# Decay-gate products stacked over 96 rows, and first q and k projections started on three of six token tiles

## The reference, cut to what matters

```python
h = rmsnorm(x, norm_mix)
proj = h @ w_in                      # qa, ka, va, qb, kb, vb, og, gf, gb, ma, mb
logg_f = jax.nn.log_sigmoid(gf @ w_gate_f + b_gate_f) / GATE_TAU   # gf: [T, 16], w_gate_f: [16, 4 heads x 128]
logg_b = jax.nn.log_sigmoid(gb @ w_gate_b + b_gate_b) / GATE_TAU
o_f = gla_chunked(qb, kb, vb, logg_f, False)                      # per head, chunks of 64 tokens
o_b = flip(gla_chunked(flip(qb), flip(kb), flip(vb), flip(logg_b), True))
...
x = x + mix @ w_out
x = x + hier_moe(rmsnorm(x, norm_moe), ...)                       # 32 experts, two of them per token
return rmsnorm(x, norm_final)
```

## Time and profile before

| | us |
|---|---|
| median of 3 runs | 1326.04 |
| lowest, highest run | 1317.42, 1728.16 |
| the profiled execution | 1316.45 |
| its span, first to last instruction | 1314.3 |
| TensorE busy in the span | 1190.0 |
| VectorE, ScalarE, GpSimd busy | 645.2, 599.3, 338.8 |

### The profile page before, as it was taken

The page is one execution under the profiler, slowest core; times in us unless marked ns, Lnnn a source line. Parts: engine busy times, 40 slices in busy tenths (PEclk is TensorE's granted clock), DMA queues, the critical chain, the costliest instruction groups (busy, mean ns, idle before and its releaser), DMA issues.

```text
span 1314.3 us, 18331 instructions
## 1 busy us (share of the span) xinstructions
PE 1190.0 (91%) x7184; PEld 1059.7 (81%) x7184; DVE 645.2 (49%) x1056; ACT 599.3 (46%) x994; POOL 338.8 (26%) x214
## 2 busy tenths in 40 slices
PE   5999999998999999999999999889399999999960
PEld 3998898797877878899999999889377887777750
DVE  5001512327554444355302112325498998888857
ACT  6133645534534344133212213122467888877843
POOL 1221120121111112021112024230134554444510
PEclk8999999997899999999999999899689999999995
DMA  7621101322111111111121211501679999999917
GB/s 253 196 65 32 33 5 48 107 79 61 33 33 34 32 33 32 33 45 54 53 64 42 77 60 64 182 16 65 251 289 373 366 369 367 343 366 350 349 62 288
DMA packets 89941, 184.11 MB, mean 140 GB/s; under 512 B 14009, under 2 KB 65357, under 8 KB 81678
## 3 DMA queue, kind: packets, MB, share of 16 engines
q1 hardware_dynamic: 79486, 167.16, 35.7%
q0 software_dynamic: 10384, 15.95, 3.4%
HBM read 179.32 MB, written 28.65 MB: 158 GB/s over the span
## 4 chain that ended last, share of the span: by engine, by line
PE 69%; DVE 10%; DMA 7%; ACT 7%; issue 5%; POOL 1%; SPq 0%; POOLq 0%; ACTq 0%; DVEq 0%
PE bank L1256 16%; PE bank L1258 15%; PE bank L1257 15%; DMA raw_gu<-in_w_exp_up 5%; PE bank L1443 2%; PE bank L1442 2%; PE bank L1441 2%; PE bank L1390 2%; PE bank L1321 2%; ACT w_hi L1006 2%; PE bank L1365 2%; PE bank L1343 1%; PE bank L1428 1%; PE bank L1387 1%; PE bank L1304 1%
## 5 line engine op out<-in xcount | busy, mean ns | idle before, releaser
L881 POOL TENSOR_TENSOR w_lo<-raw,w_hi 128x2048 fp32r<-128x2048 f32 (+2 forms) x37 | 152.9, 4133 | 673.4 <-ACT w_hi L1006 673.3
L1256 PE MATMUL bank<-hT_hi,w_hi 128*128 128x384 f32 (+1 forms) x592 | 202.9, 343 | 4.0 <-DVE hT_lo L1580 4.0
L1257 PE MATMUL bank<-hT_lo,w_hi 128*128 128x384 f32 (+1 forms) x592 | 199.7, 337 | 0.0
L1258 PE MATMUL bank<-hT_hi,w_lo 128*128 128x384 f32 (+1 forms) x592 | 199.6, 337 | 0.0
L995 ACT ACTIVATE hi_gu<-raw_gu 128x2048 fp32r<-128x2048 f32 x64 | 122.4, 1918 | 62.9 <-issue 51.5
L1844 DVE TENSOR_TENSOR lo_gu<-raw_gu,hi_gu 128x2048 fp32r<-128x2048 f32 x64 | 146.3, 2287 | 6.3 <-ACT hi_gu L995 6.1
L1256 PE MATMUL bank<-w_hi,hT_hi 128*128 128x256 f32 x432 | 126.3, 292 | 0.0
L1257 PE MATMUL bank<-w_lo,hT_hi 128*128 128x256 f32 x432 | 123.4, 286 | 0.0
L1258 PE MATMUL bank<-w_hi,hT_lo 128*128 128x256 f32 x432 | 123.4, 286 | 0.0
L1006 ACT ACTIVATE w_hi<-raw 128x2048 fp32r<-128x2048 f32 (+2 forms) x42 | 73.6, 1752 | 103.0 <-PE bank L1258 103.0
L1256 PEld LDWEIGHTS bank<-hT_hi,w_hi 128*128 128x128 f32 (+1 forms) x592 | 111.3, 188 | 9.1 <-DVE hT_lo L1580 4.4
(11 more groups left out here) (291 smaller groups left out, 2544.7 us busy)
## 6 DMA issues: line engine op xcount, KB each, us to landing
raw_gu<-in_w_exp_gate SPq DMA_DIRECT2D x32, 1024.0 KB, 10.9
raw_gu<-in_w_exp_up SPq DMA_DIRECT2D x32, 1024.0 KB, 13.7
raw_down<-in_w_exp_down SPq DMA_DIRECT2D x32, 1024.0 KB, 14.8
raw<-in_w_in SPq DMA_DIRECT2D x25, 1024.0 KB, 5.6
y_pair<-y_d SPq DMA_DIRECT2D x12, 512.0 KB, 9.0
raw<-in_w_in SPq DMA_DIRECT2D x8, 512.0 KB, 5.8
raw<-in_w_proj_b SPq DMA_DIRECT2D x4, 1024.0 KB, 5.0
raw<-in_w_out SPq DMA_DIRECT2D x4, 1024.0 KB, 5.2
```

The lines of the kernel that those rows point to most:

```text
L881: pool.tensor_tensor(w_lo[:, g % 2, 0:kb, 0:n], raw[:, g % 2, 0:kb, 0:n], w_hi[:, g % 2, 0:kb, 0:n].bitcast(F32), ALU.subtract).then_inc(w ...
L1256: pe.matmul(out, l_hi, r_hi, start=j == 0, stop=False)
L1257: pe.matmul(out, l_hi, r_lo, start=False, stop=False)
L1258: ins = pe.matmul(out, l_lo, r_hi, start=False, stop=j == n - 1)
```

## The change

The gate's weight columns are loaded three times, so that its product has 96 rows: three copies of the 32. Evacuated, the rows become hi, lo and hi (ScalarE copies all 96, VectorE subtracts on the middle 32). A new step `wgz` makes the matching operand from a 96-row `wgate`: ScalarE copies all of it to `wgz`, VectorE replaces the last 32 rows by the rest. Then z is one `fp32r` matmul over 96 rows instead of a float32 matmul over 32. In the step list `wgz` stands right in front of z, and so behind the `w` step that ends the projection before it.

At the start the list is written out by hand: the first four products (q and k, token half 0) need only tiles 0 to 2 and stand between the transposes of tiles 3 to 5; the `w` steps of groups 0 and 1 move forward; group 0 is loaded before tiles 3 to 5, the replication of the bias vectors behind group 2's load. TensorE gets filler transposes of the identity (14 ahead of each of the first three tiles' transposes, 28 ahead of the first product), whose results are overwritten. The root of the norm takes its scale and bias on ScalarE, without VectorE's step.

```diff
+WARM = 14
+G2, G3 = 2 * RANK, 6 * RANK
...
-    for i in range(NT + 2):
-        if i < NT:
-            if i < NV:
-                steps.append(S(kind="vec", a=i))
-            steps.append(S(kind="norm", i=i))
-        if i == NT:
-            steps.append(S(kind="w", g=0))
-        if i >= 2:
-            steps += [S(kind="hT", i=i - 2, half=h) for h in range(2)]
-    steps.append(S(kind="w", g=1))
-    steps += proj("q", 0) + proj("k", 0) + proj("v", 0)
+    hT = lambda i: [S(kind="hT", i=i, half=h) for h in range(2)]
+    norm = lambda i: [S(kind="norm", i=i)]
+    vec = lambda a: [S(kind="vec", a=a)]
+    q, k = proj("q", 0), proj("k", 0)
+    early, late = ([s for s in q + k if s.kind == "w" or s.s == half] for half in range(2))
+    early = [s for s in early if s.kind == "ws"]
+    steps += vec(0) + norm(0) + vec(1) + norm(1) + hT(0) + vec(2) + norm(2) + hT(1) + [S(kind="w", g=0)] + hT(2)
+    steps += norm(3) + early[0:1] + hT(3) + norm(4) + [S(kind="w", g=1)] + vec(3) + early[1:2] + norm(5) + vec(4)
+    steps += hT(4) + early[2:3] + hT(5) + early[3:4] + late + proj("v", 0)
...
-    other = v[3:] + z
+    other = v[3:] + [S(kind="wgz", h=0)] + z
...
-        steps += other[i:i + 1]
+        steps += other[0:2] if i == 3 else other[0:1]
+        del other[0:2 if i == 3 else 1]
...
-            steps += [S(kind="z", h=h + 1, d=d, s=s) for d in range(2) for s in range(2)]
+            steps += [S(kind="wgz", h=h + 1)] + [S(kind="z", h=h + 1, d=d, s=s) for d in range(2) for s in range(2)]
...
-                return [(w_in[:, C_GATE:C_GATE + 2 * RANK], KD, 0, 2 * RANK)]
+                return [(w_in[:, C_GATE:C_GATE + G2], KD, c0, G2) for c0 in range(0, G3, G2)]
...
-            for i in range(1, NT):
+            for i in range(1, NT // 2):
+                sp.dma_start(xin[:, i, :], x_rows(i)).then_inc(x_in[i], 16)
+            load_group(0)
+            for i in range(NT // 2, NT):
                 sp.dma_start(xin[:, i, :], x_rows(i)).then_inc(x_in[i], 16)
...
+                    if s.g + 1 < len(glist):
+                        if s.g:
+                            need(sp, E_, wlo_done, s.g)
+                        load_group(s.g + 1)
+                    if s.g == 1:
                         replicate_vectors()
...
-                        need(pool, E_, mm, find(kind="z", h=h - 1)[-1].job + 1)
-                    pool.dma_start(wgate[0:RANK, 0, :], ...
-                    pool.dma_start(wgate[RANK:2 * RANK, 1, :], ...
+                        need(pool, E_, wgz_done, h)
+                    for c0 in range(0, G3, G2):
+                        pool.dma_start(wgate[c0:c0 + RANK, 0, :], ...
+                        pool.dma_start(wgate[c0 + RANK:c0 + G2, 1, :], ...
...
-                    need(act, E_, var_done, i + 1)
-                    act.activation(std[:, i:i + 1], rstd[:, i:i + 1], ACT.Sqrt).then_inc(std_done, 1)
+                    need(act, E_, consts, 2)
+                    need(act, E_, sq_done, i + 1)
+                    act.activation(std[:, i:i + 1], ss[:, i:i + 1], ACT.Sqrt, scale=1.0 / D, bias=eps[:, 0:1])\
+                       .then_inc(std_done, 1)
...
+                elif k == "wgz":
+                    need(act, E_, wg_in, 96 * (s.h + 1))
+                    if s.h:
+                        need(act, E_, mm, find(kind="z", h=s.h - 1)[-1].job + 1)
+                    act.activation(wgz[:, :, :], wgate[:, :, :], ACT.Copy).then_inc(wgz_hi, 1)
+                elif k == "ws" and s.dest[0] == "gate":
+                    need(act, E_, mm, s.job + 1)
+                    act.activation(gT[:, s.s * HALF:(s.s + 1) * HALF], bank(s.job)[0:G3, 0:HALF], ACT.Copy).then_inc(gT_hi_done, 1)
...
+                    if s.half == 0 and s.i < NT // 2:
+                        for _ in range(WARM):
+                            pe.transpose(b_[:, 0:P], ident[:, :], ident[:, :])
                     need(pe, E_, xn_done, s.i + 1)
...
+                    if g == 0 and s.b == 0 and s.s == 0:
+                        for _ in range(2 * WARM):
+                            pe.transpose(b_[:, 0:P], ident[:, :], ident[:, :])
...
-                        evac_done(pe, E_, last_hT)
+                        first_half = k == "ws" and s.s == 0
+                        evac_done(pe, E_, find(kind="hT", i=NT // 2 - 1)[-1].job if first_half else last_hT)
...
-                    need(pe, E_, wg_in, 32 * (s.h + 1))
+                    need(pe, E_, wgz_done, s.h + 1)
                     evac_done(pe, E_, last_of_group[gnum["gate", 0]])
-                    ins = pe.matmul(b_[:, 0:HALF], wgate[:, s.d, :], gT[:, s.s * HALF:(s.s + 1) * HALF],
+                    ins = pe.matmul(b_[:, 0:HALF], wgz[:, s.d, :], gT[:, s.s * HALF:(s.s + 1) * HALF],
                                     start=True, stop=True)
...
+                if k == "wgz":
+                    need(dve, E_, wgz_hi, s.h + 1)
+                    dve.tensor_tensor(wgz[2 * G2:G3, :, :], wgate[2 * G2:G3, :, :], wgz[2 * G2:G3, :, :].bitcast(F32),
+                                      ALU.subtract).then_inc(wgz_done, 1)
+                elif k == "ws" and s.dest[0] == "gate":
+                    tok = slice(s.s * HALF, (s.s + 1) * HALF)
+                    need(dve, E_, gT_hi_done, s.s + 1)
+                    dve.tensor_tensor(gT[G2:2 * G2, tok], b_[G2:2 * G2, 0:HALF], gT[G2:2 * G2, tok].bitcast(F32),
+                                      ALU.subtract).then_inc(dve_evac, 1)
...
-                    need(dve, E_, sq_done, i + 1)
-                    dve.tensor_scalar(rstd[:, i:i + 1], ss[:, i:i + 1], 1.0 / D, EPS, ALU.mult, ALU.add).then_inc(var_done, 1)
```

More of the change, by code:

```diff
@@ L264, in plan @@
     jobs = Jobs()
-    act_evacuates = {"q", "k", "v", "gate", "qkb", "vb", "og", "ma", "mb"}
+    act_evacuates = {"q", "k", "v", "qkb", "vb", "og", "ma", "mb"}
     last_of_group = {}
@@ L392, in build @@
         ptg = at("ptg", [P, 2, P], F32, 146)
-        wgate = at("wgate", [2 * RANK, 2, P], F32, 147)
+        wgate = at("wgate", [G3, 2, P], F32, 147)
+        wgz = const("wgz", [G3, 2, P], F32R)
         zt = at("zt", [P, 2, T], F32, 160)
-        gT = at("gT", [2 * RANK, T], F32, 166)
+        gT = at("gT", [G3, T], F32R, 166)
         et = at("et", [P, 2, T], F32, 169)
@@ L522, in build @@
         raw_in = [sem("raw_in0"), sem("raw_in1")]
-        wg_in = sem("wg_in")
+        wg_in, wgz_hi, wgz_done, gT_hi_done = sem("wg_in"), sem("wgz_hi"), sem("wgz_done"), sem("gT_hi_done")
         vec_out, rep_out, table_in = sem("vec_out"), sem("rep_out"), sem("table_in")
@@ L529, in build @@
         hi_done = sem("hi_done")
-        sq_done, var_done, std_done, xn_done = sem("sq_done"), sem("var_done"), sem("std_done"), sem("xn_done")
+        sq_done, std_done, xn_done = sem("sq_done"), sem("std_done"), sem("xn_done")
         att_out, att_in = ([sem(f"att_out{a}") for a in (1, 2)], [sem(f"att_in{a}") for a in (1, 2)])
@@ L697, in group_shape @@
             name, _ = glist[g]
-            return (2 if name == "pa" else KD), (2 * RANK if name == "gate" else GW)
+            return (2 if name == "pa" else KD), (G3 if name == "gate" else GW)
         def dve_splits(g):
@@ L711, in _, with load_group @@
             E_ = "sp"
+            def load_group(g):
+                for src, kb, c0, n in group_parts(g):
+                    sp.dma_start(raw[:, g % 2, 0:kb, c0:c0 + n],
+                                 src.rearrange("(k p) n -> p k n", p=P)).then_inc(raw_in[g % 2], 16)
             sp.dma_start(onehot[:, :, :], A["const_buckets"].rearrange("b (a n) -> b a n", a=NV)).then_inc(rel_in, 16)
@@ L891, in _ @@
                     else:
-                        need(pool, E_, mm, find(kind="z", h=h - 1)[-1].job + 1)
-                    pool.dma_start(wgate[0:RANK, 0, :], A["w_gate_f"][0][:, h * DK:(h + 1) * DK]).then_inc(wg_in, 16)
-                    pool.dma_start(wgate[RANK:2 * RANK, 1, :], A["w_gate_b"][0][:, h * DK:(h + 1) * DK]).then_inc(wg_in, 16)
+                        need(pool, E_, wgz_done, h)
+                    for c0 in range(0, G3, G2):
+                        pool.dma_start(wgate[c0:c0 + RANK, 0, :], A["w_gate_f"][0][:, h * DK:(h + 1) * DK]).then_inc(wg_in, 16)
+                        pool.dma_start(wgate[c0 + RANK:c0 + G2, 1, :], A["w_gate_b"][0][:, h * DK:(h + 1) * DK]).then_inc(wg_in, 16)
                 elif s.kind == "gstat":
@@ L1042, in _ @@
                             ins.then_inc(act_evac, 1)
-                        elif name == "gate":
-                            act.activation(gT[:, tok], b_[0:2 * RANK, 0:HALF], ACT.Copy).then_inc(act_evac, 1)
                         elif name == "qkb":
@@ L1262, in _ @@
                 k = s.kind
-                if k in ("w", "vst", "norm", "natural", "comb", "mix", "soft", "cumul", "decay", "decay2", "ob", "gstat", "mixT", "norm2", "route"):
+                if k in ("w", "vst", "norm", "natural", "comb", "mix", "soft", "cumul", "decay", "decay2", "ob", "gstat", "mixT", "norm2", "route", "wgz"):
```

(4 more changed lines are left out.)

## The result

The changed kernel took 1343.03 us, the median of four runs (1340.37 to 1347.28), against 1321.73 for the kernel before in the same comparison: a ratio of 1.018, 95% interval [1.014, 1.022]. The 1321.73 is a median that holds one slow run of 1728.16 us, which the ratio leaves out, so the ratio isn't that of the two medians. The forecast was 1333, 1.3% longer. The direction was right, and so was the place of the larger part, the z products; the size was 7 us short by the profiled execution (1340.37) and 10 by the median, and most of what is missing lies in attention. The span is 23.5 us longer than that of the earlier trace rows.

What follows compares the result with a forecast made beforehand. TensorE was taken as the bound, holding 69% of the chain, with waits in some stages. 1316.45 + 1.0 (gate's operands) + 18.6 (z's stalls) + 0.2 (head 0) - 3.0 (start) = 1333 us, range 1318 to 1347.

Steps and rivals of the forecast that it cites:

- z's stall (part 2): Heads 1 to 3: `wgz` subtraction held by GpSimd's `w_lo`, z 7.4 us late, first state product 6.2 later, +18.6 in all.
- the second rival: States and `vb` products of heads 1 to 3: clock stays low behind each stall, 4 us a head, 1345; chance 0.13.
- z itself: Gate's z products in each head: four matmuls at 0.173 instead of 0.69 us save 2.1 a head if nothing waits.
- The first rival: z in heads 1 to 3: subtraction not held, z 3.3 late, first state some 1.4 later, 1319; chance 0.13.
- The gate's operands (part 1): Attention: wider gate split and added VectorE subtraction partly show in its short waits, +1.0, bounds 0 and 2.5.
- The start (part 3): First eight q/k products: first near 22 us, third 35.7, eighth ending 61.7 against 66.3; taken as -3.0 (+0.5 to -4.6).
- The fourth rival: Start: first products begin earlier but nothing ends earlier, 1336; chance 0.13.
- the third rival: Start: fillers stay at the lower clock level, the lead becomes a loss of 4.3 to 4.5, 1341; chance 0.11.
- Head 0: Head 0's mixing steps: subtraction held in place of the addition, mixing follows, z faster; +0.2 (-0.5 to +1.5).

Runs made afterwards that it cites:

- gate_only: Only the gate's part of the change (three copies, `wgz`, one-pass z) in the kernel before, with its old start: 1342.29 us, ratio 1.021.
- wgz_early: The whole change with the `wgz` step of heads 1 to 3 moved ahead of the `qkb` projection: 1328.07 us, ratio 1.010 to the kernel before.
- no_fill: The changed kernel without any filler transposes: 1343.17 us.
- start_only: Only the new start, fillers and norm's root on ScalarE in the kernel before, with the old gate: 1322.59 us, ratio 1.002.
- after_again: The changed kernel executed once more, unedited, for a second trace: 1345.37 us.
- w_behind: `wgz_early` with the `w` step that ends a `qkb` projection moved behind z and `kot`: 1318.99 us, ratio 0.997 to the kernel before.

## Why the prediction was right and wrong

- **z's stall (part 2).** Right in place, holder and size. z 7.4 us late forecast, 7.29 measured; z at 0.35 each, 0.41 measured; the first state product 6.2 later, 6.39 in head 2, and by ScalarE's rows the heads are 6.39, 6.40 and 8.24 longer (18.6 forecast, 21.0 in sum; 18.6 in `gate_only`, by the table's column of heads). Head 3's larger figure is the second rival at work in one head: there the windows show 13.6 us at the lower level behind the stall (478 to 492 us). The rule of the Trainium skill that fits is in "SBUF — State Buffer" (SBUF: two separate sides): a VectorE operation with two SBUF inputs and a GpSimd operation that reads SBUF exclude each other for a whole instruction. The trace agrees: the subtraction took 4.52 us beside GpSimd's 4.49, and 0.42 without it.
- **z itself.** "Four save 2.1 us a head if nothing waits": they save 1.97 (`wgz_early`), but nothing of it arrives unless the `w` step is moved, and then 2.4 us in three heads. Inside the stall's sum the step was sound: there `w_hi` is long done when z starts, and the first state product follows z by 4.99 us instead of 5.89. The first rival (no hold, 1319) counted on it for the first state product too (z 3.3 late, the state only 1.4), and `wgz_early`, at 1328, shows no such gain.
- **The gate's operands (part 1).** This is the step that failed: +1.0 forecast with bounds of 0 and 2.5, 7.7 measured in its stage. The operations are within the bounds (GpSimd's split takes 1.82 us where 0.73 + 1.4 was forecast, ScalarE's grows by 0.43, and 0.2 to 0.8 us are left for their effect). What was put at nothing, without a reason, was the clock, some 7.5 us: the windows of before showed 1.00 all through attention, and I took that for a property of the stage. One execution's trace couldn't show that its pauses stood so close to a fall; a second one of the same kernel already has 3.4 us at the lower level.
- **The start (part 3).** First product near 22 forecast, 22.48 measured; third 35.7 and 36.44; eighth evacuation 3.0 earlier, 3.81 in the first profile. But the executions divide: 62.61, 65.14, 65.90 (`no_fill`), 66.47 and 66.86 in the profiles with both parts, 61.66 in `start_only`. In the last three of the five the level fell at the third product (38 to 43 us), as the working had it at even odds; the pause there was 1.8 us, 2.5 forecast. The median of `start_only` gains nothing. The fourth rival (nothing ends earlier) is thus true of a part of the executions.
- **Fillers.** In the first profile they ran at 0.23 us each in the first tile and 0.13 from the second, as forecast; in `after_again`, `wgz_early` and `w_behind` the second 14 took 3.25 us as well, and the level rose with the third (1.69). A part of the third rival is in that: its slow second tile, not its slow first product. So transposes brought the level up here, as in the kernel before. The rule of "TensorE: Matmul & The Clock Gate" in the Trainium skill that the prediction weighed (Part 4: PE-mode transpose), that transposes don't engage the full clock, isn't borne out by these rows. The trace lists the fillers as matmuls, so it doesn't show whether they ran in the mode that the page means. The sum by that rule, 1341, is near the measured time for another reason.
- **Head 0.** +0.2 forecast, -0.3 measured. The subtraction is held there too (4.52 us) and nothing is lost.
- **The sum.** By its own terms: attention 7.7 for 1.0, the heads 21.0 for 18.6, the start -3.8 for -3.0, head 0 -0.3 for 0.2, is 24.6 for 16.8, and the stages behind the heads give 1.1 of it back. 1343 lies within the range, which held it by the second rival's width; but that rival's place, the stages behind each stall, isn't where most of the missing time went.

## What to carry to other kernels

Before an operation is made shorter, read what ends last behind it: here z fell from 2.84 to 0.87 us and the engine behind it stood at another step. Moving that one, which also drew a product of another projection into the pause, gave the 0.5% that the shorter operation didn't. A small VectorE operation with both inputs in SBUF belongs where GpSimd isn't in a long one, also where a list of steps makes it look adjacent and cheap. Where a stage has many pauses of a microsecond, a clock of 1.00 in one trace is one outcome among several; read a second execution before pricing the clock at nothing, and set the mean granted clocks of all executions beside their times.

## What the hardware showed that was not expected

The same pause of 1.06 us in the same code kept the upper level in one execution and lost it in another (914 us). At one place of attention a pause of 0.70 us kept the level in three profiles and lost it in four, and one of 1.11 lost it in six and kept it in one. A start that was 1.7 to 4.8 us earlier or 2.9 later went with 10.2 to 13.6 us at the lower level in a stage 60 us further on in which nothing was edited, 4.2 to 6.0 us of time. The unedited kernel's runs spread over 1312.5 to 1326.9 us, and their mean granted clock goes with it: 0.949 to 0.951 above 1324 us, 0.952 to 0.962 below 1322.
